# Paged value matmuls of a decode step: four pages to four groups of 32 PSUM partitions

## The chip, the cores and the metric

The kernel runs on one core of one Trainium2 chip. The metric is the device time of one execution, in microseconds (us). Shown are three runs of the kernel before; the median counts.

## The reference

One inference step of a two-layer decoder runs a prompt of 1024 positions and 8 sample sequences through the same weights. The change touches one part of layer 0, the forgetting attention of the 8 samples (FoX, 8 heads of 64), whose keys and values lie in pages of 128 positions:

```
def _fox_sample(q, k_new, v_new, logf_new, k_pool, v_pool, lf_pool, page_table):
    ...
    v_all = jnp.concatenate([v_pool[page_table].reshape(b, past, h, d).astype(v_new.dtype), v_new], axis=1)
    ...
    sc = jnp.einsum('bqhd,bkhd->bhqk', q, k_all).astype(jnp.float32) * (FOX_HD ** -0.5)
    sc = sc + c[:, :, past:, None] - c[:, :, None, :]
    ...
    p = jax.nn.softmax(sc, axis=-1).astype(v_all.dtype)
    return jnp.einsum('bhqk,bkhd->bqhd', p, v_all).reshape(b, l, h * d)
```

Here b is 8 samples, h is 8 heads, d is 64, and the past is 16 pages a sample, 128 pages in all. The change concerns the last line: probabilities times value pages.

## The kernel before, in words

The program is written by hand for five engines, each with its own list of instructions, joined by semaphores. SyncE (SP) issues most loads, TensorE (PE) does the matmuls, VectorE (DVE), ScalarE (ACT) and GpSimd (POOL) the rest. The instruction order on every engine is the order in which the code is written.

Layer 0 projects the inputs (`pe_ab_in`), turns and pools (`pe_naturals`, `pe_pool`), and then comes the stage of the change, `pe_attention` (L1133) with `act_attention`, `dve_attention`, `pool_attention` and, on SP, `sp_pages` (L944). Two pieces of work are woven together there:

- **Prompt attention** in 64 tiles (8 heads by 8 query blocks), pipelined over three rounds of a loop in n: round n has `pe_scores(n+1)` (L849), `pe_turn(n-1)` (eight transposes at most, L894) and `pe_values(n-2)` (L911). A tile of block i covers 128(i+1) keys, so its cost grows and falls with n modulo 8.
- **Sample attention** over the pages. Pages stay in `kpage`, a ring of 4 slots with 2 pages each; a step u fills one slot. SP's `fill` waits until step u-4 has been used (`pages_used`), reads two page numbers from `page_idx` (L953) and issues two loads of 256 KB (L959). Steps 0 to 63 are key pages: POOL multiplies them (L981), DVE reduces them (L987), in rounds 0 to 47. In round 48 the softmax over all samples makes the probabilities `sc`. Steps 64 to 127 are value pages, in rounds 50 to 65, four steps (eight pages) a round, after the prompt tile's own matmuls.

A sample has 16 value pages, so two rounds make one sample. `pe_sample_values` (L1052) multiplies a page of 128 positions by 512 columns with the 8 heads' probabilities of this sample and sums the 16 pages in `ps[0:8, 7, :]`, 8 partitions of PSUM bank 7. Each head's row then holds all 512 columns, of which its own 64 are wanted: `dve_sample_own` (L1065) multiplies by the mask `own` (ones in head h's 64 columns), `pe_sample_columns` (L1073) sums the 8 rows into 4 columns of 128 with ones as the moving operand, and `dve_sample_columns` (L1079) copies them out. The next sample's first page waits for that copy, since all use bank 7.

All of these matmuls are float32. The trace has two records, each with a weight load of its own, for each matmul of the program: 256 for the 128 pages.

POOL builds `own` in round 8 (`pool_own`, L1110) in 8 partitions of `w_pl`, which is free by then.

Of the kernel before, what the change touches and what calls it, by code (L numbers as in the profile page):

```python
# [24 lines left out]
ALU = mybir.AluOpType  # L25
# [6 lines left out]
P = 128  # L32
# [29 lines left out]
def hybrid_step(nc, A, O):  # L62

    with ExitStack() as ctx:
# [7 lines left out]
        def sb(name, shape, dt=F32, at=None):  # L72
            return (at or ctx).enter_context(nc.sbuf_tensor(name, shape, dt))

        def scratch(name, shape):
# [24 lines left out]
            "p (a n) -> p a n", a=4)  # L100
        smx = sb("smx", [P, DECB, 2, MH])
        sel_b = sb("sel_b", [MH * DECB, DECB])
        smr = sb("smr", [P, 4, DECB, MH])
        dskip = sb("dskip", [P, DC])
        s_new = sb("s_new", [P, 4, DECB])
# [15 lines left out]
        w_pl = sb("w_pl", [P, 4, P], F32, rest)  # L121
        lf_pg = sb("lf_pg", [P, DECB, NPG, FH], F32, rest)
        ulast = sb("ulast", [PBUF, FW], F32, rest)
        own = w_pl[0:FH].rearrange("p g n -> p (g n)")
        rest.close()
        rest = ExitStack()
        xin = sb("xin", [P, 2, D], F32, rest)
# [100 lines left out]

        STEPS = {
            "pe": ("colsT_ready", "gate_logits0", "gate_logits1", "gate_logits2", "gate_turned", "gate_sums",  # L230
                    "gate_rowsT", "stateT_ready", "ulastT_ready", "s_natT_ready", "s_values_ready",
                    "convT_turned", "dt_logits0", "dt_logits1", "dt_logits2", "dt_turned", "dt_sums",
                    "dt_rowsT", "tailT_ready", "s_bcT_ready", "lastT_ready", "wmT_turned", "v_rowT"),
            "act": ("gate_rows0", "gate_rows1", "gate_rows2", "gate_ln", "gate_token_rows", "ulast_ready",
                    "s_nat_ready", "sc_exp", "convT_ready", "dt_rows0", "dt_rows1", "dt_rows2", "dt_ln",
                    "dt_token_rows", "s_decay_ready", "ctail_ready", "s_bc_ready", "last_ready", "g_mean_sq",
                    "g_std", "v_row_ready", "rms_rstd"),
            "dve": ("inv_cnt_ready", "sel_b_ready", "gate_biased", "logf_ready", "c_ready", "new_scores",
                    "sc_cleared", "s_max_ready", "sc_shifted", "s_sum_ready", "sc_ready", "dt_biased",
                    "da_ready", "dec_diff", "g_var", "wmT_ready", "xdt_s"),  # L240
            "pool": ("own_ready", "s_max_all", "s_sum_all"),
        }
        pe_steps, act_steps, dve_steps, pool_steps = (sem(f"{e}_steps") for e in ("pe", "act", "dve", "pool"))
        marked = {e: 0 for e in STEPS}
# [805 lines left out]


        def pe_sample_values(pe, u):  # L1052
            b, slot = u // (NPG // 2), u % 4
            pe.wait_ge(page_loaded[slot], 32 * ((N_STEP + u) // 4 + 1))
            if u == 0:
                pe.wait_ge(dve_steps, step("sc_ready"))
                pe.wait_ge(sem("suffix_copied"), 8)
            if u % (NPG // 2) == 0 and b:
                pe.wait_ge(sem("s_own_step"), 2 * b)
            for e in range(2):  # L1060
                g = 2 * (u % (NPG // 2)) + e
                mm = pe.matmul(ps[0:FH, 7, :], sc[:, b, :, g], kpage[:, slot, e], start=(g == 0), stop=(g == NPG - 1))  # L1062
            mm.then_inc(pages_used, 1)

        def dve_sample_own(dve, b):  # L1065
            if b == 0:
                dve.wait_ge(pool_steps, step("own_ready"))
# [42 lines left out]
        def pool_own(pool):  # L1110
            then = chain(pool, "pool")
            pool.wait_ge(sem("pool_copied"), 4)
            then(pool.memset(own, 1.0))
            then(pool.affine_select(out=own, in_=own, compare_op=ALU.is_ge, fill=0.0, base=0,
                                    pattern=[[1, FW]], channel_multiplier=-FD))
            pool.affine_select(out=own, in_=own, compare_op=ALU.is_ge, fill=0.0, base=FD - 1,
                               pattern=[[-1, FW]], channel_multiplier=FD).then_inc(pool_steps, mark("own_ready"))

        def pool_attention(pool):
            pool.sem_inc(pages_used, 4)  # L1120
# [12 lines left out]
        def pe_attention(pe):  # L1133
            pe.wait_ge(set_free[0], G1["ab_u"])
            pe.wait_ge(act_steps, step("s_nat_ready"))
            pe.wait_ge(sem("v_copied"), NT)
            pe.wait_ge(act_steps, step("ulast_ready"))
            pe.wait_ge(sem("pool_copied"), 4)
            pe_scores(pe, 0)
            for n in range(N_ATT + 2):  # L1140
                if n + 1 < N_ATT:
                    pe_scores(pe, n + 1)
                if 1 <= n <= N_ATT:
                    pe_turn(pe, n - 1)
                if n >= 2:
                    pe_values(pe, n - 2)
                if 8 <= n < 12:
                    pe_suffix(pe, n - 8)
                if sample_done(n) is not None:
                    pe_sample_columns(pe, sample_done(n))  # L1150
                for u in value_steps(n):
                    pe_sample_values(pe, u)
            pe_sample_columns(pe, DECB - 1)
            pe_sample_new(pe)

        def act_attention(act):
            for n in range(N_ATT + 2):
                if n < N_ATT:
                    act_exp(act, n)
                    if n % NT == NT - 1 and n // NT + 2 < FH:  # L1160
                        act_load_c(act, n // NT + 2)
                if 1 <= n <= N_ATT:
                    act_turn(act, n - 1)
                if n >= 2:
                    act_out(act, n - 2)
                if n == KEYS_END:
# [1396 lines left out]
```

## Time and profile before

| | us |
|---|---|
| three runs | 4037.15, 4042.88, 4042.89 |
| median | 4042.88 |
| span of the profiled execution | 4042.7 |
| prompt tiles with key pages, about 315 to 502 | 187 |
| prompt tiles with value pages, 528.5 to 696.5 | 168 |

The profile is one execution; its span is 0.2 us under the median of the runs, and its own time is one of that size. TensorE is busy for 89% of the span and holds 73% of the chain of work that ended last. Layer 0's output projection follows the stage of the change and starts on TensorE at 702.4 us. Where the profile gives a granted clock, 1.00 is 2.4 GHz and 0.50 is 1.2 GHz; a stretch in between has some of both.

### The profile page before, as it was taken

Reading aid. Unit: us, or ns where it says so; the run is one execution under the profiler, and the core shown is the slowest. Engines: PE = TensorE matmul, PEld = TensorE weight load, DVE = VectorE, ACT = ScalarE, POOL = GpSimd, SP = SyncE. Lnnn points to the kernel's source line nnn. Section 1 sums busy time; section 2 is a strip of 40 time slices with the busy share of each in tenths; the row PEclk is TensorE's granted clock in tenths of the full one; section 3 lists DMA queues with packets and bytes.
Section 4 is the critical chain, followed back from the end, with each engine's and each line's share of the span. In section 5 each row is a group of like instructions: output and inputs, shape, how many; then the busy total and the mean of one; then the engine's idle time right before and its main releaser. Section 6 shows DMA issues by size and latency. Waiting matters only on the chain.

```text
span 4042.7 us, 55900 instructions
## 1 busy us (share of the span) xinstructions
PE 3584.0 (89%) x21060; PEld 3248.2 (80%) x21060; DVE 1514.9 (37%) x2160; ACT 1005.0 (25%) x1325; POOL 586.3 (15%) x367
## 2 busy tenths in 40 slices
PE   7978899979988999999779986668899799999996
PEld 6955533969778999999778975658896799999996
DVE  1159922442444212222431438654343522221225
ACT  2123321142323101111232323432332311111112
POOL 2337700210022000000220014002100300000003
PEclk9977899999999999999889998889999899999997
DMA  2235655133411111111122112331352111111111
GB/s 82 54 107 162 185 162 171 57 109 106 144 42 34 45 47 47 42 47 43 30 68 71 47 44 89 126 120 52 104 171 75 30 47 47 43 45 47 47 35 54
DMA packets 370178, 311.19 MB, mean 77 GB/s; under 512 B 23520, under 2 KB 312721, under 8 KB 369923
## 3 DMA queue, kind: packets, MB, share of 16 engines
q1 hardware_dynamic: 354351, 291.40, 23.9%
q10 hardware_dynamic: 11620, 17.77, 1.3%
q0 software_dynamic: 4096, 0.53, 0.2%
q8 instruction: 71, 1.16, 0.1%
q14 instruction: 40, 0.33, 0.0%
HBM read 283.46 MB, written 26.51 MB: 77 GB/s over the span
## 4 chain that ended last, share of the span: by engine, by line
PE 73%; DVE 11%; issue 5%; DMA 4%; POOL 3%; ACT 3%; SPq 2%; ACTq 0%; DVEq 0%; POOLq 0%
PE ps L302 62%; PE ps L1062 2%; POOL kpage L981 2%; PE ps L1494 1%; PE ps L1516 1%; DVE spl_w L287 1%; PE ps L1472 1%; DVE acc L2111 1%; PE ps L600 1%; DMA acc<-spill_d 1%; DVE x L1289 1%; SPq L953 1%; DMA raw_w<-in_w_xv 1%; ACT x L1303 1%; POOL x L1295 1%
## 5 line engine op out<-in xcount | busy, mean ns | idle before, releaser
L302 PE MATMUL ps<-xs,spl_w 128*128 128x344 f32 x12528 | 2006.8, 323 | 53.4 <-DVE spl_w L287 25.2
L302 PEld LDWEIGHTS ps<-xs,spl_w 128*128 128x128 f32 x12528 | 2000.8, 190 | 57.5 <-issue 27.2
L287 DVE TENSOR_TENSOR spl_w<-raw_w,spl_w 128x1024 fp32r<-128x1024 f32 x268 | 327.1, 1220 | 839.5 <-ACT spl_w L283 835.5
L302 PE MATMUL ps<-hs,spl_w 128*128 128x344 f32 x3168 | 512.5, 325 | 27.5 <-DVE hs L1707 27.5
L302 PEld LDWEIGHTS ps<-hs,spl_w 128*128 128x128 f32 x3168 | 510.9, 192 | 29.0 <-issue 29.0
L283 ACT CAST spl_w<-raw_w 128x1024 fp32r<-128x1024 f32 x268 | 279.4, 1042 | 390.6 <-PE ps L302 362.6
L1243 POOL MEMSET sum_x<- 128x1032 f32 x6 | 5.9, 982 | 1739.2 <-DVE hs L1707 1374.0
L1705 DVE TENSOR_TENSOR sum_x<-sq,ps 128x1032 f32<-128x1032 f32 x44 | 54.1, 1229 | 351.5 <-PE ps L302 351.5
L1251 POOL TENSOR_TENSOR sum_x<-sum_x,x 128x1032 f32<-128x1032 f32 x48 | 115.9, 2414 | 474.7 <-DVE x L1211 188.1
L1295 POOL TENSOR_TENSOR x<-x,sum_x 128x1032 f32 x48 | 138.5, 2893 | 200.4 <-DVE x L1289 200.4
L981 POOL TENSOR_TENSOR kpage<-kpage,qb 128x1024 f32<-128x1024 f32 x64 | 156.3, 2459 | 65.5 <-DMA kpage<-in_cache_fox_k 65.3
L1689 ACT CAST hs<-sum_x 128x1032 f32 (+1 forms) x44 | 46.4, 1055 | 472.2 <-DVE sum_x L1705 472.2
L1211 DVE SCALAR_TENSOR_TENSOR x<-x,ps 128x1032 f32 (+1 forms) x48 | 58.9, 1228 | 267.9 <-PE ps L302 267.9
L1229 ACT ACTIVATE sq<-x 128x1032 f32 (+1 forms) x48 | 51.2, 1067 | 420.7 <-DVE x L1211 233.9
L1220 DVE TENSOR_TENSOR sum_sq<-sum_sq,sq 128x1032 f32<-128x1032 f32 x48 | 106.7, 2223 | 92.6 <-ACT sq L1229 60.3
L1213 DVE TENSOR_TENSOR x<-x,ps 128x1032 f32 (+1 forms) x40 | 49.2, 1229 | 242.4 <-PE ps L302 242.4
L317 PE MATMUL ps<-xs,spl_w 128*128 128x344 f32 x432 | 78.8, 342 | 62.1 <-DVE xs L1307 62.1
L302 PE MATMUL ps<-mem_s,spl_w 128*128 128x256 f32 x768 | 103.6, 294 | 32.6 <-DVE spl_w L287 17.0
L1685 ACT ACTIVATE sq<-ps 128x1032 f32<-128x1032 f32 x44 | 45.4, 1032 | 339.9 <-PE ps L302 336.2
L302 PEld LDWEIGHTS ps<-mem_s,spl_w 128*128 128x128 f32 x768 | 98.0, 199 | 39.4 <-DVE spl_w L287 19.8
L317 PEld LDWEIGHTS ps<-xs,spl_w 128*128 128x128 f32 x432 | 73.8, 203 | 67.9 <-issue 47.2
L1062 PE MATMUL ps<-kpage,sc 128*8 128x512 f32 x256 | 113.4, 592 | 5.3 <-DMA kpage<-in_cache_fox_v 2.8
(344 smaller groups left out, 3224.1 us busy)
## 6 DMA issues: line engine op xcount, KB each, us to landing
kpage<-in_cache_fox_k SPq DMA_DIRECT2D x128, 256.0 KB, 2.9
kpage<-in_cache_fox_v SPq DMA_DIRECT2D x128, 256.0 KB, 2.9
raw_w<-in_w_gate SPq DMA_DIRECT2D x44, 512.0 KB, 3.8
raw_w<-in_w_up SPq DMA_DIRECT2D x44, 512.0 KB, 3.8
mkv<-in_cache_mem_k SPq DMA_DIRECT2D x16, 1024.0 KB, 8.2
mkv<-in_cache_mem_v SPq DMA_DIRECT2D x16, 1024.0 KB, 5.1
raw_w<-in_w_down SPq DMA_DIRECT2D x32, 512.0 KB, 3.8
raw_w<-in_w_in_cd SPq DMA_DIRECT2D x28, 512.0 KB, 3.8
```

The lines of the kernel that those rows point to most:

```text
L283: act.copy(spl_w[:, s, 0], raw_w[:, s]).then_inc(hi_ready, 1)
L287: dve.tensor_tensor(spl_w[:, s, 1], raw_w[:, s], spl_w[:, s, 0].bitcast(F32), ALU.subtract).then_inc(lo_ready, 1)
L302: mm = pe.matmul(ps[:, 3 * s + t, 0:width], spl_w[:, s, a, k], part[:, k, width * t:width * (t + 1)], start=(k == 0 and step == 0), stop=( ...
L317: mm = pe.matmul(ps_set[s][:, t], spl_w[:, s, a, k], act_in[:, b, k, TB * t:TB * (t + 1)], start=(k == 0 and step == 0), stop=(k == DC - 1 ...
L981: pool.tensor_tensor(kpage[:, slot], kpage[:, slot], qb[:, b % 2].unsqueeze(1).to_broadcast([P, 2, FW]), ALU.mult).then_inc(sem("keys_mult ...
L1062: mm = pe.matmul(ps[0:FH, 7, :], sc[:, b, :, g], kpage[:, slot, e], start=(g == 0), stop=(g == NPG - 1))
L1211: ins = dve.scalar_tensor_tensor(out=xm, in0=xm, scalar=ALPHA, in1=ps_set[s], op0=ALU.mult, op1=ALU.add)
L1220: dve.tensor_tensor(sum_sq[:], sum_sq[:], sq[:], ALU.add).then_inc(sem("sq_used"), 1)
L1229: act.activation(sq[:], chunk(x, 2 * i + s), ACT.Square).then_inc(sem("sq_ready"), 1)
L1251: pool.tensor_tensor(sum_x[:], sum_x[:], chunk(x, 2 * i + s), ALU.add).then_inc(sem("sum_x_ready"), 1)
L1295: pool.tensor_tensor(xk, xk, sum_x[:], ALU.add).then_inc(sem("ln_shifted"), 1)
L1705: dve.tensor_tensor(blocks(sum_x[:]), blocks(sq[:]), ps_set[1], ALU.mult).then_inc(set_free[1], 1)
```

## The change

Four pages go through TensorE together. Page j of the four writes PSUM partitions 32j to 32j+31 of bank 7. For that the stationary operand has 32 columns, the 8 heads of four samples (the sample's own and three others), where it had the 8 heads of one. Each group of 32 partitions sums 4 of the sample's 16 pages. Afterwards the mask `own` covers 128 partitions, head h's 64 columns repeated in every eighth row, and `sel_row[:, b % 4]`, a column that is 1 in the 8 rows of sample b in each group and 0 in the 24 others, takes the place of the ones in the summing matmul.

A call of `pe_sample_values` now takes two slots: it waits for both, issues four matmuls and frees the first slot after the second and the second after the fourth. SP's program is unchanged.

Added are two small DVE operations at the start (`sel_row`, `head_of`) and, in round 20, one matmul (`pe_own`) and one ACT copy of 128x512 (`act_own`), which spread POOL's 8 rows of the mask over 128 partitions. The first value page now waits for ACT's copy, and DVE's first masking too, where it waited for POOL.

```diff
-        own = w_pl[0:FH].rearrange("p g n -> p (g n)")
+        own = w_pl[:].rearrange("p g n -> p (g n)")
...
+            dve.tensor_reduce(sel_row[:], ident[:].rearrange("p (j m h) -> p m j h", j=4, h=FH), AX.XY, ALU.add
+                              ).then_inc(dve_steps, mark("sel_row_ready"))
+            dve.tensor_copy(head_of[:].rearrange("p (r h) -> p r h", h=FH),
+                            ident[0:FH, 0:FH].unsqueeze(1).to_broadcast([FH, P // FH, FH])
+                            ).then_inc(dve_steps, mark("head_of_ready"))
...
         def pe_sample_values(pe, u):
-            b, slot = u // (NPG // 2), u % 4
-            pe.wait_ge(page_loaded[slot], 32 * ((N_STEP + u) // 4 + 1))
+            b = u // (NPG // 2)
+            for v in (u, u + 1):
+                pe.wait_ge(page_loaded[v % 4], 32 * ((N_STEP + v) // 4 + 1))
             if u == 0:
+                pe.wait_ge(act_steps, step("own_ready"))
...
-            for e in range(2):
-                g = 2 * (u % (NPG // 2)) + e
-                mm = pe.matmul(ps[0:FH, 7, :], sc[:, b, :, g], kpage[:, slot, e], start=(g == 0), stop=(g == NPG - 1))
-            mm.then_inc(pages_used, 1)
+            for j in range(4):
+                g = 2 * (u % (NPG // 2)) + j
+                mm = pe.matmul(ps[32 * j:32 * (j + 1), 7, :], sc[:, 4 * (b // 4):4 * (b // 4 + 1), :, g],
+                               kpage[:, (u + j // 2) % 4, j % 2], start=(g < 4), stop=(g >= NPG - 4))
+                if j % 2:
+                    mm.then_inc(pages_used, 1)
...
-            dve.tensor_tensor(qb[0:FH, b % 2], ps[0:FH, 7, :], own, ALU.mult).then_inc(sem("s_own_step"), 1)
+            dve.tensor_tensor(qb[:, b % 2], ps[:, 7, :], own, ALU.mult).then_inc(sem("s_own_step"), 1)
...
-                mm = pe.matmul(ps[:, 7, c:c + 1], qb[0:FH, b % 2, P * c:P * (c + 1)], ones[0:FH, 0:1], start=True, stop=True)
+                mm = pe.matmul(ps[:, 7, c:c + 1], qb[:, b % 2, P * c:P * (c + 1)], sel_row[:, b % 4:b % 4 + 1], start=True, stop=True)
...
+        def pe_own(pe):
+            pe.wait_ge(pool_steps, step("own_rows"))
+            pe.wait_ge(dve_steps, step("head_of_ready"))
+            pe.wait_ge(sem("suffix_copied"), 8)
+            pe.matmul(ps[:, 7, :], head_of[:], own[0:FH], start=True, stop=True).then_inc(pe_steps, mark("own_spread"))
+
+        def act_own(act):
+            act.wait_ge(pe_steps, step("own_spread"))
+            act.copy(own, ps[:, 7, :]).then_inc(act_steps, mark("own_ready"))
...
-                for u in value_steps(n):
+                if n == 20:
+                    pe_own(pe)
+                for u in value_steps(n)[::2]:
                     pe_sample_values(pe, u)
```

On TensorE, round 52 of the stage stood so before: the sums of the sample that has just ended (L1076), then four steps of two pages (L1062), each with a wait of its own, then the scores of the next tile (L849).

```order
L1076 MATMUL ps<-ones,qb 128x1 [waits s_own_step]
L1076 MATMUL ps<-ones,qb 128x1 x3
L1062 MATMUL ps<-kpage,sc 8x512 [waits s_own_step,page_loaded0]
L1062 MATMUL ps<-kpage,sc 8x512
L1062 MATMUL ps<-kpage,sc 8x512 [waits page_loaded1]
L1062 MATMUL ps<-kpage,sc 8x512
L1062 MATMUL ps<-kpage,sc 8x512 [waits page_loaded2]
L1062 MATMUL ps<-kpage,sc 8x512
L1062 MATMUL ps<-kpage,sc 8x512 [waits page_loaded3]
L1062 MATMUL ps<-kpage,sc 8x512
L849 MATMUL ps<-proj 128x512 [waits scores_shifted]
```

The same round in the changed kernel, where L1087 is the sum, L1071 the values and L856 the scores:

```order
L1087 MATMUL ps<-sel_row,qb 128x1 [waits s_own_step]
L1087 MATMUL ps<-sel_row,qb 128x1 x3
L1071 MATMUL ps<-kpage,sc 32x512 [waits s_own_step,page_loaded1,page_loaded0]
L1071 MATMUL ps<-kpage,sc 32x512 x3
L1071 MATMUL ps<-kpage,sc 32x512 [waits page_loaded3,page_loaded2]
L1071 MATMUL ps<-kpage,sc 32x512 x3
L856 MATMUL ps<-proj 128x512 [waits scores_shifted]
```

There are as many matmuls as before, with 32 output rows for 8, in two groups of four pages in place of four of two; the waits of two slots have moved to the head of each group.

In round 20, in the stage of the key pages, TensorE's list has one new row (L1135) between the tile's values (L918) and the next tile's scores (L856); before, the second followed the first.

```order
L901 MATMUL ps<-ident,prob 128x128 x3
L918 MATMUL ps<-pT,proj 64x128 [waits out_copied,pT_copied]
L918 MATMUL ps<-pT,proj 64x128 x2
L1135 MATMUL ps<-w_pl,head_of 128x512 [waits suffix_copied,dve_steps,pool_steps]
L856 MATMUL ps<-proj 128x512 [waits scores_shifted]
L856 MATMUL ps<-proj 128x384
```

Behind that row the tile's next scores wait for POOL's mask rows and for DVE's copies out of bank 7, both of rounds up to 12.

## Rows read from the trace of the kernel before

**Rows 1.** The page: span, TensorE's busy time, and the chain that ended last.

```profile
span 4042.7 us, 55900 instructions
...
PE 73%; DVE 11%; issue 5%; DMA 4%; POOL 3%; ACT 3%; SPq 2%; ACTq 0%; DVEq 0%; POOLq 0%
PE ps L302 62%; PE ps L1062 2%; POOL kpage L981 2%; PE ps L1494 1%; PE ps L1516 1%; DVE spl_w L287 1%; PE ps L1472 1%; DVE acc L2111 1%; PE ps L600 1%; DMA acc<-spill_d 1%; DVE x L1289 1%; SPq L953 1%; DMA raw_w<-in_w_xv 1%; ACT x L1303 1%; POOL x L1295 1%
```

**Rows 2.** Groups by line, value stretch: count | busy us, mean ns | idle before.

```profile
L1062 PE MATMUL ps<-kpage,sc 128*8 128x512 f32 x256 | 113.4, 592 | 5.3 <-DMA kpage<-in_cache_fox_v 2.8 <-DVE s_sum L1081 2.4
L1062 PEld LDWEIGHTS ps<-kpage,sc 128*8 128x8 f32 x256 | 22.0, 92 | 84.0 <-issue 73.8 <-DMA kpage<-in_cache_fox_v 10.2
...
L1071 DVE TENSOR_TENSOR qb<-ps,w_pl 8x512 f32<-8x512 f32 x8 | 5.4, 679 | 73.6 <-PE ps L1062 73.6
```

**Rows 3.** TensorE in order of time: start, us, what, [idle before].

```profile
528.49 7.04 PE L1062 MATMUL ps<-kpage,sc 128*8 128x512 f32 x16
...
567.94 1.98 PE L849 MATMUL ps<-proj 64*128 64x512 f32 x4
...
571.89 1.05 PE L1076 MATMUL ps<-ones,qb 8*128 8x1 f32 x8
573.29 7.03 PE L1062 MATMUL ps<-kpage,sc 128*8 128x512 f32 x16 [0.35 <-DVE s_sum L1081]
...
611.63 1.12 PE L849 MATMUL ps<-proj 64*128 64x512 f32 x2
...
613.41 1.05 PE L1076 MATMUL ps<-ones,qb 8*128 8x1 f32 x8
```

**Rows 4.** SP in order of time: all issues of value pages behind the first eight.

```profile
531.25 160.93 SPq L959 DMA_DIRECT2D kpage<-in_cache_fox_v  x120
```

**Rows 5.** SP's waits, 505 to 702 us: total, times, longest.

```profile
SPq L953 <- PE ps L1062: 21.6, 5, 17.1
```

**Rows 6.** Chain in order of time, 505 to 705 us: two turns of SP's loop, the end.

```profile
671.21 0.25 issue
...
681.71 0.25 issue
...
691.84 2.69 DMA kpage<-in_cache_fox_v
694.58 1.90 PE ps L1062 x4
```

**Rows 7.** TensorE in layer 1, two heads that meet in 64 columns each.

```profile
2456.61 0.38 PE L2147 MATMUL ps<-xbc,hprev 128*64 128x128 f32 x2
2456.83 0.44 PE L2145 MATMUL ps<-acc,xdt 128*64 128x128 f32 x4
2457.05 0.27 PE L2147 MATMUL ps<-xbc,hprev 128*64 128x128 f32 x1
2457.10 0.27 PE L2145 MATMUL ps<-acc,xdt 128*64 128x128 f32 x1
2457.16 0.27 PE L2147 MATMUL ps<-xbc,hprev 128*64 128x128 f32 x1
2457.21 0.27 PE L2145 MATMUL ps<-acc,xdt 128*64 128x128 f32 x1
```

**Rows 8.** Stretches: length, PE, PEld, DVE, ACT, POOL busy, granted clock, DMA share, GB/s.

```profile
315.00:502.00 187.00, 155.84 (x679) 98.66 (x679) 174.04 (x349) 70.22 (x162) 143.36 (x63) 0.79 0.57 175
528.00:697.00 169.00, 163.21 (x567) 57.87 (x565) 28.94 (x106) 25.78 (x57) 0.16 (x1) 1.00 0.63 187
702.00:706.00 4.00, 3.63 (x13) 3.66 (x14) 4.00 (x5) 4.00 (x5) 0.00 (x0) 0.50 0.00 0
```

**Rows 9.** ACT's copies of 128x512 out of PSUM: min, median, max ns, first and last start.

```profile
L724 ACT COPY kst<-ps x8: 585/585/586, 239.1 to 250.7; 128x512 f32<-128x512 f32 x8
```

**Rows 10.** VectorE in order of time at the start of the program.

```profile
5.69 0.12 DVE L452 TENSOR_REDUCE sel_b<-ident 32x8 f32<-32x32 f32 x1
50.00 1.23 DVE L287 TENSOR_TENSOR spl_w<-raw_w,spl_w 128x1024 fp32r<-128x1024 f32 x1 [44.19 <-ACT spl_w L283]
```

More of the change, by code:

```diff
@@ L102, in hybrid_step @@
         sel_b = sb("sel_b", [MH * DECB, DECB])
+        sel_row = sb("sel_row", [P, 4])
+        head_of = sb("head_of", [FH, P])
         smr = sb("smr", [P, 4, DECB, MH])
@@ L230, in hybrid_step @@
             "pe": ("colsT_ready", "gate_logits0", "gate_logits1", "gate_logits2", "gate_turned", "gate_sums",
-                    "gate_rowsT", "stateT_ready", "ulastT_ready", "s_natT_ready", "s_values_ready",
+                    "gate_rowsT", "stateT_ready", "ulastT_ready", "s_natT_ready", "own_spread", "s_values_ready",
                     "convT_turned", "dt_logits0", "dt_logits1", "dt_logits2", "dt_turned", "dt_sums",
@@ L234, in hybrid_step @@
             "act": ("gate_rows0", "gate_rows1", "gate_rows2", "gate_ln", "gate_token_rows", "ulast_ready",
-                    "s_nat_ready", "sc_exp", "convT_ready", "dt_rows0", "dt_rows1", "dt_rows2", "dt_ln",
+                    "s_nat_ready", "own_ready", "sc_exp", "convT_ready", "dt_rows0", "dt_rows1", "dt_rows2", "dt_ln",
                     "dt_token_rows", "s_decay_ready", "ctail_ready", "s_bc_ready", "last_ready", "g_mean_sq",
                     "g_std", "v_row_ready", "rms_rstd"),
-            "dve": ("inv_cnt_ready", "sel_b_ready", "gate_biased", "logf_ready", "c_ready", "new_scores",
+            "dve": ("inv_cnt_ready", "sel_b_ready", "sel_row_ready", "head_of_ready", "gate_biased", "logf_ready", "c_ready", "new_scores",
                     "sc_cleared", "s_max_ready", "sc_shifted", "s_sum_ready", "sc_ready", "dt_biased",
                     "da_ready", "dec_diff", "g_var", "wmT_ready", "xdt_s"),
-            "pool": ("own_ready", "s_max_all", "s_sum_all"),
+            "pool": ("own_rows", "s_max_all", "s_sum_all"),
         }
@@ L1059, in pe_sample_values @@
                 pe.wait_ge(sem("s_own_step"), 2 * b)
-            for e in range(2):
-                g = 2 * (u % (NPG // 2)) + e
-                mm = pe.matmul(ps[0:FH, 7, :], sc[:, b, :, g], kpage[:, slot, e], start=(g == 0), stop=(g == NPG - 1))
-            mm.then_inc(pages_used, 1)
+            for j in range(4):
[4 more added lines that the diff above has]
+                    mm.then_inc(pages_used, 1)
         def dve_sample_own(dve, b):
             if b == 0:
-                dve.wait_ge(pool_steps, step("own_ready"))
+                dve.wait_ge(act_steps, step("own_ready"))
             dve.wait_ge(pages_used, N_STEP + 4 + (NPG // 2) * (b + 1))
@@ L1112, in pool_own @@
             pool.wait_ge(sem("pool_copied"), 4)
-            then(pool.memset(own, 1.0))
-            then(pool.affine_select(out=own, in_=own, compare_op=ALU.is_ge, fill=0.0, base=0,
+            rows = own[0:FH]
+            then(pool.memset(rows, 1.0))
+            then(pool.affine_select(out=rows, in_=rows, compare_op=ALU.is_ge, fill=0.0, base=0,
                                     pattern=[[1, FW]], channel_multiplier=-FD))
-            pool.affine_select(out=own, in_=own, compare_op=ALU.is_ge, fill=0.0, base=FD - 1,
-                               pattern=[[-1, FW]], channel_multiplier=FD).then_inc(pool_steps, mark("own_ready"))
+            pool.affine_select(out=rows, in_=rows, compare_op=ALU.is_ge, fill=0.0, base=FD - 1,
+                               pattern=[[-1, FW]], channel_multiplier=FD).then_inc(pool_steps, mark("own_rows"))
+        def pe_own(pe):
[6 more added lines that the diff above has]
+            act.copy(own, ps[:, 7, :]).then_inc(act_steps, mark("own_ready"))
         def pool_attention(pool):
@@ L1165, in act_attention @@
                     act_out(act, n - 2)
+                if n == 20:
+                    act_own(act)
                 if n == KEYS_END:
```

## The prediction

> **What bounds the kernel now.** I read the page first. TensorE is busy for 89% of a span of 4042.7 us and holds 73% of the chain, but the line that the change speeds up, L1062, has only 2% of the chain [rows 1]. So I left the whole program and looked at its stretch, 528 to 697 us, by groups. There L1062 has 256 records and 113.4 us of 169, at the full clock, and TensorE is busy for 163 of the 169 [rows 2, 8]. By that view the stretch is TensorE's. The timeline gives the real rate: 16 records in 7.04 us, so 0.44 us from one start to the next (the mean of 592 ns counts a tail that overlaps the next), 0.88 us a page and 1.76 us a step of two pages [rows 3]. All 128 pages are 112.6 us.
>
> The next view turns this over. SP issued the last 120 value pages from 531.25 on, over 160.9 us with the last issue's own 0.34 us, 160.6 from first start to last [rows 4]. One turn of its loop is eight pages: two marks of a turn stand at 671.21 and 681.71, 10.50 us apart [rows 6]. Fifteen turns are 157.5 us; the last turn ends at its eighth issue and not at the next turn's first, 1.7 us less, so 155.8. SP therefore lost only 160.6 - 155.8 = 4.8 us. The view of its waits agrees: 21.6 us on L1062 in five waits, of which one of 17.1 us lies before 531, while the ring was full and nothing had been used; 4.5 us are left for the other four [rows 5]. So two engines are almost level: SP takes 10.5 us for the eight pages of a round, and TensorE 7.0 us for their matmuls beside 1.8 to 5.4 us for the rest of the round. The ring of four slots hides the one behind the other. The chain ends on SP: last load issued at 691.84, landed 2.7 us later, two pages' matmuls of 1.90 us [rows 6], then the mask and the sums. DMA is no third limit, at 0.63 of its time [rows 8].
>
> **The change part by part.** The numbers go against this execution's own span of 4042.7 us; the median of the three runs is 4042.88, so I write the result against that.
>
> *The four matmuls.* A page keeps its two records, 0.43 to 0.44 us apart. The trace of before has no four matmuls in four groups of 32 columns. Its nearest row is in layer 1, where one head's matmuls write partitions 0 to 63 and the next head's 64 to 127: two records of one head take 0.38 us, each 0.27 long, 0.11 apart, but where two heads meet the starts are 0.05 to 0.06 apart, 2457.05, 2457.10, 2457.16, 2457.21 [rows 7]. Both halves stream at their own full rate. With four such groups, four pages take 2 x 0.44 + 0.15 (the tail of the last) = 1.05 us; two at a time 4 x 0.44 + 0.15 = 1.9; one after the other 8 x 0.44 + 0.15 = 3.7. I take 1.1, since [rows 7] show independent column groups at work, and keep 3.7 as the far end. The stage's L1062 time falls from 113 to some 35 us. The wider weight load (32 columns for 8, 92 ns before [rows 2]) lies under the matmul ahead.
>
> *What this is worth.* Not 78 us, for SP is unchanged: 155.8 us from its first issue to its last. The most that can be gained is: SP's stalls, 4.8; the first slots come free after 1.1 us and not 1.76, 0.7; and behind the last landing four pages take 1.1 us and not two pages 1.9, 0.8. Together **6.3 us**, if no new stall comes.
>
> *The pairing.* A group needs two slots, and the ring has two groups. SP takes 5.25 us for a group of four pages. From the landing of a group's last page to the moment at which SP wants its first slot back I count 5.25 (the next group) + 1.3 (its next issue) - 2.9 (landing) - 1.0 (530.25, when the first step ended, to the issue at 531.25 [rows 3, 4]) = 2.6 us. TensorE is away for the tile's own matmuls meanwhile: 3.95 us in the longest round (567.94 to 571.89), and in every second round 1.05 for the sums and 0.35 for their copy, 5.35 in all [rows 3]. A group that lands 5.25 us after the one before was landed and used 1.1 later is used 1.1 + 5.35 + 1.1 - 5.25 = 2.3 us after landing. That is just under 2.6: at the full clock the pairing costs nothing or a few tenths.
>
> *The clock.* In the value stretch TensorE never rested and had 1.00. In the stretch of the key pages, with the same prompt tiles and pauses between them, it had 0.79 on the mean [rows 8], that is 42% of the time at 1.2 GHz. After the change a round is 10.5 us with about 2.9 + 0.7 + 2.2 = 5.8 us of work on TensorE, so pauses come back, and I expect the same fall. At 1.2 GHz a round of the longest kind takes 2 x (3.95 + 1.05 + 2.1) + 0.35 = 14.5 us, 4.0 more than SP's 10.5; of the shortest even kind (1.78 us from 611.63 to 613.41) 2 x (1.78 + 1.05 + 2.1) + 0.35 = 10.2. By the mean of the two ends the seven rounds with sums would be 1.85 us too long each, 13 us in all, and 28 if all were of the longest kind; rounds without sums fit on the mean (12.1 and 7.8 by the same ends). I take 17 us if the whole stretch ran so, nearer the mean. At 42% of it 7 us; but short slow spells are in part taken up by the ring, and a round at the full clock catches up. Bounds 0 and 7; I take half, **3.5 us**.
>
> *The rest.* `pe_own` is one matmul of 512 columns, 0.9 us by the same spacing, and ACT's copy 0.59 us [rows 9]. They stand in the key stretch, where POOL and DVE are busy 77% and 93% [rows 8] and TensorE and ACT wait; the next scores and the next exponential are behind them, so between 0 and 1.5 us, say **1**. The mask on DVE has 128 partitions for 8 with the same 512 columns, 0.68 us [rows 2]; eight sums keep their shape but for the rows. The two small DVE operations fall into a wait of 44 us that ends at 50.00, and one like them took 0.12 us [rows 10]: nothing. The new wait of the first value page on ACT's copy ended some 30 rounds ago. The projection behind the stretch starts at 0.50 of the clock already [rows 8], so a low clock at the end costs it nothing more.
>
> *Sum.* -6.3 + 3.5 + 1 = -1.8 us: 4042.9 - 1.8 = **4041.1 us**. A measurement of this kernel can tell about 0.2% from no change, 8.1 us; this is well inside.
>
> **The rivals.**
>
> *The clock holds.* If the matmuls of four pages count as work enough and 1.00 stays, the whole 6.3 us come, less the 1 us: 4037.6. For it: with some 5.8 us of work in 10.5, the pauses are cut in short pieces. Against it: in the key stretch TensorE is busy for 156 of 187 us and the clock fell all the same [rows 8]. Still within 0.2% of before.
>
> *One after the other.* The change doesn't do what it says if column groups with a common set of rows run in turn. Then TensorE has its old work and the coarser ring: a group lands 5.25 - 3.7 = 1.6 us behind the use of the last, and its first step is used 5.35 + 1.76 - 1.6 = 5.5 us after landing, 2.9 too late, in the longest round; 0.7 in the shortest; over seven such rounds some 12 us of stalls for the 4.8 of before, and 1.8 us more at the end: +9, 4052. It decides as soon as four pages take over 2.5 us. What [rows 7] show speaks against it, though with two groups and not four. The Trainium skill, "TensorE: Matmul & The Clock Gate", Part 3 under "The mechanism", speaks for it: a weight load overlaps matmuls in flight only where the row group differs, and here all four pages use all 128 rows. By that rule each of eight loads would show too, with 0.09 us apiece a group of 4.4 us (an estimate), and the time would be this rival's and not the sum's. The trace does not agree: a load that waited for the other half's matmuls, 0.27 us long, would keep the starts apart, and they come 0.05 us apart [rows 7].
>
> *The clock stays low.* If 1.2 GHz lasts nearly through the stretch, the 17 us above stand against 6.3 gained, with 1 for the key stretch: +12, 4055. It decides where rounds of 12 to 14 us follow each other. For it: in the key stretch the low clock went on while TensorE was busy 156 of 187 us. Against it: such a stretch is busy all the time, and the same clock rose again and again there.
>
> *TensorE is the limit after all.* Then the 78 us saved would show: 3965. SP's times speak against it [rows 4, 6]; it would have to issue twice as fast. The skill's "TensorEngine Tiling (Array Packing)", under "Theoretical Speedup", gives up to 4x for 32 columns; that is this rival's gain on L1062, and by my sum it is there and not worth having.
>
> **How the numbers follow.** Forecast 0.52, the clock holds 0.18, one after the other 0.13, the clock stays low 0.14, TensorE the limit 0.03. The forecast's own range, with clock costs of 0 to 7 and pages two at a time, is 4036 to 4047. To leave out no more than 2 in 10 it must take in 4052 and most of the slow clock: 4035 to 4054. Faster by over 0.2%: the last rival and a little of the second, 0.07. Slower: most of the two slow ones, 0.20. The rest, 0.73, is within.
>
> **What would show it.** Right: SP's 120 issues in 156 to 161 us, with TensorE idle before the value matmuls and a DMA named as the releaser; starts of four pages about 0.1 us apart; the clock between 0.6 and 0.9. Wrong: starts of the value matmuls 0.44 us apart throughout; SP's waits on them over 10 us behind the first; or an SP loop whose turn is well off 10.5 us.

## The result, and the profile after

The changed kernel takes 4056.92 us (median of 20 runs, 4049.34 to 4066.28), the kernel before 4042.89 on the same chip (20 runs, 4032.93 to 4051.63). The ratio is 1.0035, with a 95% interval of 1.0028 to 1.0042: **slower by 14 us**. The prediction said no measurable change, 4041.1, with a range up to 4054. The profiled execution has a span of 4056.0 us, 13.3 more than before.

The value matmuls first. TensorE's groups by line, 528 to 715 us (columns as in [rows 2]), and VectorE's masking in the view by line:

```profile
L1071 PE MATMUL ps<-kpage,sc 128*32 128x512 f32 x256 | 52.2, 916 | 49.6 <-DMA kpage<-in_cache_fox_v 47.1 <-DVE s_sum L1092 2.4
```

```profile
L1082 DVE TENSOR_TENSOR qb<-ps,w_pl x8: 690/691/693, 547.6 to 712.3; 128x512 f32<-128x512 f32 x8
```

The 256 records are busy for 52.2 us where they were 113.4 [rows 2]: the part that was to become quick did. In front of them TensorE now waits 47.1 us for loads, where it was 2.8. The mask costs 0.69 us for 0.68, as forecast.

TensorE in order of time, two pieces of the stretch (columns as in [rows 3]):

```profile
569.52 1.94 PE L1071 MATMUL ps<-kpage,sc 128*32 128x512 f32 x8 [2.63 <-DMA kpage<-in_cache_fox_v]
571.39 3.78 PE L856 MATMUL ps<-proj 64*128 64x512 f32 x4
...
578.42 1.05 PE L1087 MATMUL ps<-sel_row,qb 128*128 128x1 f32 x8
579.83 1.95 PE L1071 MATMUL ps<-kpage,sc 128*32 128x512 f32 x16 [0.35 <-DVE s_sum L1092]
...
588.54 1.94 PE L1071 MATMUL ps<-kpage,sc 128*32 128x512 f32 x8 [3.98 <-DMA kpage<-in_cache_fox_v]
593.64 1.94 PE L1071 MATMUL ps<-kpage,sc 128*32 128x512 f32 x8 [3.16 <-DMA kpage<-in_cache_fox_v]
```

At the full clock eight pages take 1.95 us (579.83), where 16 records took 7.04 [rows 3]; at half of it four pages take 1.94. So four groups of columns do run beside each other. The Trainium skill, "TensorE: Matmul & The Clock Gate", Part 3 under "The mechanism", lets a weight load overlap only matmuls of another row group; that rule, taken alone, would have these four pages, which share all rows, run in turn. The trace doesn't agree: 1.95 us for eight pages has no room for it. But the quick groups now wait for loads (2.63, 3.98, 3.16), and the prompt's scores behind one of them take 3.78 us for four records where the same shape took 1.98 [rows 3].

The clock by stretches says why: the stretch of [rows 8], then one of 120 us that lies inside the value stretch of every kernel below (length, busy PE, PEld, DVE, ACT, POOL, granted clock, DMA share, GB/s):

```profile
528.00:697.00 169.00, 126.55 (x540) 61.14 (x538) 28.91 (x105) 26.49 (x59) 2.35 (x1) 0.64 0.58 171
537.00:657.00 120.00, 89.50 (x363) 41.37 (x363) 20.76 (x78) 17.74 (x41) 0.00 (x0) 0.63 0.60 180
```

Before, the same two stood at 1.00. At a mean of 0.64, TensorE is at 1.2 GHz for 72% of the time ((1 - 0.64) / 0.5). The same page of the Trainium skill, Part 1 under "HAM oscillation — how this bites in real kernels", tells of a kernel whose short groups of matmuls wait for loads in between and start each time at the low clock. The trace agrees in part: the three groups behind waits of 2.6 to 4.0 us take 1.94 us each, the time of the low clock, while the eight pages at 579.83, which follow prompt work and sums without a wait for loads, run at the full one.

SP, its value loads in order of time and its waits from 505 to 725 us, answers to [rows 4, 5]:

```profile
533.84 173.66 SPq L966 DMA_DIRECT2D kpage<-in_cache_fox_v  x120
```

```profile
SPq L960 <- PE ps L1071: 33.9, 8, 15.7
```

The first wait, 15.7, is the full ring before the first use. The other seven are 18.2 us, where four had 4.5. One by one they are 3.0, 3.1, 2.4, 1.1, 3.1, 5.3 and 0.2 us, and each stands before the issue that needs the slot of a new sample's first page: they fall in the seven rounds with the sums, the rounds that the prediction had found too long at 1.2 GHz. SP's loop needs 173.3 us from first start to last, 17.5 over the 155.8 of an SP that never waits: the waits account for all of it. The chain at the end, as in [rows 6]:

```profile
707.16 2.95 DMA kpage<-in_cache_fox_v
710.25 2.00 PE ps L1071 x8
712.27 0.70 DVE qb L1082
713.02 1.88 PE ps L1087 x8
```

The value stretch (first value matmul to the end of the last) lasts 180.3 us for 168.0. The 13.3 us of the span are: 3.4 by which it starts later (531.9 for 528.5), 12.3 by which it is longer, 1.1 between its end and the output projection (7.0 us for 5.9; the last sums, 713.02, take 1.88 us at the low clock, where 578.42 has 1.05 at the full one), and 3.5 less in the rest of the program: 3336.8 us for 3340.3. That rest is 3336.8 us in e5 below too, which has the matmuls of before, so the 3.5 us are not shown to be the change's.

### The profile page after: what moved, and what is told of

Its sections match the earlier page's. It is cut to its first block, busy times and chain, and to the rows that moved or that the text cites. A ratio compares the mean times of both kernels' runs of the same rounds, so it can differ in the third digit from the quotient of the medians.

```text
span 4056.0 us, 55933 instructions
## 1 busy us (share of the span) xinstructions
PE 3558.2 (88%) x21062; PEld 3255.4 (80%) x21062; DVE 1516.4 (37%) x2162; ACT 1005.7 (25%) x1326; POOL 586.3 (14%) x367
## 4 chain that ended last, share of the span: by engine, by line
PE 73%; DVE 10%; issue 5%; DMA 4%; ACT 3%; POOL 2%; SPq 2%; ACTq 0%; DVEq 0%; POOLq 0%
PE ps L304 62%; PE ps L1520 1%; PE ps L1542 1%; PE ps L856 1%; PE ps L918 1%; POOL kpage L988 1%; SPq L960 1%; DVE spl_w L289 1%; DMA raw_w<-in_w_xv 1%; DVE x L1315 1%; DVE acc L2137 1%; PE ps L607 1%; DMA acc<-spill_d 1%; PE ps L1071 1%; PE ps L1498 1%
## 5 line engine op out<-in xcount | busy, mean ns | idle before, releaser
L304 PE MATMUL ps<-mem_s,spl_w 128*128 128x256 f32 x768 | 101.4, 290 | 34.0 <-DVE spl_w L289 18.2
L856 PE MATMUL ps<-proj 64*128 64x512 f32 (+2 forms) x192 | 118.0, 740 | 1.4 <-ACT proj L819 1.3
```

Of the source, the lines that this page charges most:

```text
L304: mm = pe.matmul(ps[:, 3 * s + t, 0:width], spl_w[:, s, a, k], part[:, k, width * t:width * (t + 1)], start=(k == 0 and step == 0), stop=( ...
L856: mm = pe.matmul(score_ps[n % 2][:, k0:k1], proj[r, h // 2, P * i:P * (i + 1)], proj[r, 4 + h // 2, k0:k1], start=True, stop=True)
```

## The experiments

The theory after this reading: TensorE got quick, so it waited, so its clock fell; at 1.2 GHz the prompt tiles keep it from the pages, slots come back late, and SP, which sets the pace, loses 18 us. The rival: the pairs do it, whatever the clock (a pair is the two slots that one group of four pages waits for together, half of the ring). A second rival was the spreading of the mask. In all experiments the stretch is read from the first value matmul to the end of the last; medians and ratios stand against the kernel before, run beside it on the same chip (4037.99 us for e1 to e4, 4038.61 for e5 to e8, 4038.03 for e9 to e12). The stretch belongs to one profiled execution, the ratio to all runs; where they differ, the ratio is the verdict. Line numbers shift with the edits.

### e1: each slot by itself

```diff
-            for v in (u, u + 1):
-                pe.wait_ge(page_loaded[v % 4], 32 * ((N_STEP + v) // 4 + 1))
+            pe.wait_ge(page_loaded[u % 4], 32 * ((N_STEP + u) // 4 + 1))
...
             for j in range(4):
+                if j == 2:
+                    pe.wait_ge(page_loaded[(u + 1) % 4], 32 * ((N_STEP + u + 1) // 4 + 1))
```

> Four column groups as in the changed kernel, but each slot is waited for and freed by itself, in steps of two pages as before the change. Clock theory (in the value stretch TensorE ran at 1.2 GHz 72% of the time, so the prompt tiles between the pages took twice as long and slots came free late): the pauses stay, the granted clock stays at 0.6 to 0.75, SP waits 10 us or more on the value matmuls behind its first wait, 4050 to 4057 us. Pairing theory (two slots at once make the ring too coarse): SP's waits fall to 5 us or less, about 4040 us.

Measured: 4043.12 us, ratio 1.0016 (1.0006 to 1.0026), stretch 167.5 us. By stretch, and SP's waits:

```profile
537.00:657.00 120.00, 99.90 (x389) 41.07 (x389) 21.46 (x79) 17.81 (x40) 0.00 (x0) 0.74 0.66 192
```

```profile
SPq L960 <- PE ps L1072: 20.9, 4, 15.7
```

Without pairs SP loses 5.2 us behind its first wait for 18.2, about what it lost before the change. That is what the pairing theory had for the waits; the clock theory's 10 us and its 4050 to 4057 us did not come. But the kernel is still slower than before, and the clock stands at 0.74, so the clock isn't independent of the pairs. By the ratio about half of the loss is left. The one profile doesn't show where: its stretch is 0.5 us under that of before; the stretch starts 2.6 us later and 1.1 us more lie behind it.

### e2: the pairs at the full clock, with slow groups

```diff
-                mm = pe.matmul(ps[32 * j:32 * (j + 1), 7, :], sc[:, 4 * (b // 4):4 * (b // 4 + 1), :, g],
-                               kpage[:, (u + j // 2) % 4, j % 2], start=(g < 4), stop=(g >= NPG - 4))
+                mm = pe.matmul(ps[0:32, 7, :], sc[:, 4 * (b // 4):4 * (b // 4 + 1), :, g],
+                               kpage[:, (u + j // 2) % 4, j % 2], start=(g == 0), stop=(g == NPG - 1))
```

Mask and sums take 32 rows. All else stays, the pairs too.

> Pairs of slots as in the changed kernel, but all four pages go to the first 32 partitions one after the other, so TensorE has the streaming time of before (0.44 us a record). Clock theory: without pauses the clock stays at 1.00 in the value stretch and the time is that of before, 4040 to 4046 us, SP's waits about 5 us. Pairing theory: the clock is 1.00 too, but SP waits 12 us or more behind its first wait, about 4052 us.

Measured: 4051.27 us, ratio 1.0035 (1.0020 to 1.0049), stretch 177.6 us.

```profile
537.00:657.00 120.00, 112.18 (x379) 45.77 (x378) 22.18 (x85) 19.37 (x44) 0.00 (x0) 0.99 0.63 186
```

```profile
SPq L960 <- PE ps L1071: 29.0, 8, 16.7
```

```profile
583.97 3.65 PE L1071 MATMUL ps<-kpage,sc 128*32 128x512 f32 x8
```

Four pages in turn take 3.65 us, 3.3 times the 1.09 of four groups at this clock (the rows of e3). The clock stays at 0.99 and SP loses 12.3 us behind the first wait. This is what the pairing theory had (12 us or more, about 4052), and the clock theory's 4040 to 4046 failed. So pairs cost as much at the full clock, if TensorE is late for another reason: here too, pairing turned lateness of TensorE into lost time of SP.

### e3: filler work in the changed kernel

```diff
                 if j % 2:
                     mm.then_inc(pages_used, 1)
+            if u % 4 == 0:
+                for _ in range(3):
+                    pe.matmul(ps[0:1, 7, :], later[:, P - 1:P], proj[:, 12, 0:512], start=False, stop=False)
```

Three matmuls a round whose one column of weights is zero, so they add nothing to the sums.

> The changed kernel, and after the first group of four pages in each round three matmuls of 512 columns with a column of zeros as weights, added to partition 0 of bank 7, 2.6 us of streaming at 2.4 GHz in which TensorE otherwise waited for the next pages. Clock theory: the granted clock of the value stretch goes from 0.64 to 0.9 or more, SP's waits fall to 5 us or less, 4037 to 4044 us, so more work makes it faster. Pairing theory: more work on TensorE can only free slots later, 4057 us or more.

Measured: 4035.41 us, ratio 0.9993 (0.9984 to 1.0002), stretch 164.3 us.

```profile
537.00:657.00 120.00, 97.72 (x481) 39.47 (x482) 22.66 (x82) 19.46 (x44) 0.00 (x0) 0.94 0.67 199
```

```profile
SPq L960 <- PE ps L1071: 15.9, 1, 15.9
```

TensorE in order of time, a round of e3:

```profile
574.98 1.09 PE L1071 MATMUL ps<-kpage,sc 128*32 128x512 f32 x8 [0.40 <-DMA kpage<-in_cache_fox_v]
...
581.25 1.10 PE L1071 MATMUL ps<-kpage,sc 128*32 128x512 f32 x8 [2.39 <-DMA kpage<-in_cache_fox_v]
582.13 2.74 PE L1077 MATMUL ps<-proj,later 128*1 128x512 f32 x6
586.14 1.09 PE L1071 MATMUL ps<-kpage,sc 128*32 128x512 f32 x8 [1.26 <-DMA kpage<-in_cache_fox_v]
```

With 2.74 us of useless work a round (582.13) the ratio falls from 1.0035 to 0.9993, 0.42% or 17 us. The clock is at 0.94, SP waits for no slot behind the first, and the pairs are all still there. With e1 and e2 this says how the two work together: **with quick groups and a clock near the full one the pairs cost next to nothing; what the change brought is the low clock, which makes TensorE late, and the pairs pass the lateness on to SP.** No run has single slots at a clock of 0.63, so what the low clock costs without pairs isn't shown.

### e4: without the spreading of the mask

`pe_own` and `act_own` are left out, so rows 8 to 127 of the mask hold other data, and the samples' attention output becomes other numbers, with the same work.

> The changed kernel without spreading the mask: no matmul and no ACT copy in round 20, so rows 8 to 127 of the mask hold other numbers and the samples' attention output is not the reference's. If the spreading delayed the key stretch (its last key page was used about 3 us later than before), this is 3 to 4 us faster than the changed kernel, about 4053 us, and the value stretch starts at 528 to 529 us. If that delay was the chance of the clock in the key stretch, it is within 1 us of the changed kernel, 4056 to 4058 us.

Measured: 4057.84 us, ratio 1.0036 (1.0023 to 1.0049); the stretch starts at 535.8.

```profile
537.00:657.00 120.00, 90.01 (x368) 41.26 (x361) 20.36 (x78) 17.28 (x40) 0.00 (x0) 0.63 0.62 178
```

The loss and the clock are those of the changed kernel: the spreading is not the cause, nor of the later start. (A cost of 1 us could not be seen: the interval is 10 us wide.) The traces say the same of the start. Here are, from TensorE in order of time, the scores of one and the same prompt tile in the kernel before, the changed kernel and e2, whose program is the changed one's up to there, and then the matmul of the spreading in the changed kernel:

```profile
334.96 1.34 PE L849 MATMUL ps<-proj 64*128 64x512 f32 x4
```

```profile
339.85 1.34 PE L856 MATMUL ps<-proj 64*128 64x512 f32 x4
```

```profile
334.42 1.34 PE L856 MATMUL ps<-proj 64*128 64x512 f32 x4
```

```profile
390.19 2.07 PE L1135 MATMUL ps<-w_pl,head_of 8*128 8x512 f32 x2
```

The changed kernel was 4.9 us behind some 50 us before the spreading ran, and e2 was 0.5 us ahead with the same program.

### e9 and e10: is the low clock a habit, and does the dose count?

e9 is the changed kernel again; e10 is e3 with `range(1)` for `range(3)`.

> The changed kernel once more, unaltered, so that its own spread is known: its profiled execution had a value stretch of 180 us at 0.65 of the clock, and one execution is one draw. If the low clock is the kernel's habit and not that execution's, the stretch is again 174 to 184 us, the clock in it 0.6 to 0.75, and the ratio to the kernel before 1.002 to 1.005. If it was chance, the stretch is under 172.

> e3 with one filler matmul a round in place of three. Theory (idle time of TensorE lowers the clock): less work in the same pauses gives a clock between the 0.65 of none and the 0.95 of three, and a stretch between 180 and 164 us. Rival (it is not the work but the place of the three matmuls, behind the round's first group): the whole gain stays, 162 to 166 us.

Measured: e9 4054.11 us, ratio 1.0035 (1.0022 to 1.0049), stretch 177.1 us; e10 4042.88 us, ratio 1.0007 (0.9997 to 1.0016), stretch 174.1 us. The stretches, first e9's, then e10's:

```profile
537.00:657.00 120.00, 89.41 (x360) 42.35 (x361) 20.77 (x78) 16.85 (x39) 0.00 (x0) 0.63 0.60 181
```

```profile
537.00:657.00 120.00, 91.48 (x404) 41.95 (x404) 22.40 (x85) 19.37 (x44) 0.00 (x0) 0.77 0.63 187
```

The clock of 0.63 came again, and one filler lies between none and three in clock, stretch and time. But e10's profiled execution, 4053.51 us, is the slowest of its twelve, so its clock and stretch are not those of its median. By the ratio one filler brings 11 of the 17 us, and its interval overlaps that of e3: that more work gives more is likely from the clocks, 0.63, 0.77 and 0.94, and not settled by the times.

### e8: filler and single slots together

e1 and e3 in one kernel, the filler behind every second group.

> The filler matmuls of e3 together with the single slots of e1. Theory: at the full clock the pairing costs nothing, so this stands within 2 us of e3 (ratio to the kernel before 0.998 to 1.000), its stretch at 162 to 165 us. Rival, clock and pairing are two separate costs that add: it stands 6 to 9 us under e3.

Measured: 4036.20 us, ratio 0.9999 (0.9988 to 1.0010), stretch 161.9 us.

```profile
537.00:657.00 120.00, 103.33 (x482) 41.64 (x481) 23.74 (x87) 19.89 (x45) 0.00 (x0) 1.00 0.69 200
```

```profile
531.38 156.38 SPq L966 DMA_DIRECT2D kpage<-in_cache_fox_v  x120
```

Level with e3, as the theory had it; two costs that add would have shown 6 to 9 us. SP's 156.0 us from first start to last are the 155.8 of the prediction's SP that never waits, and the stretch is 6.1 us under that of before: this is the ceiling. In the time it isn't seen: the ratio allows for a gain of at most 0.12%.

### e5 to e7: SP's limit taken away

For value steps 4 to 63 SP loads the first page of a slot, and POOL the second on its own queue, with semaphores of its own (some others are shared to make room). e5 is the kernel before with this edit, e6 the changed kernel, e7 is e1 with it:

```diff
-                    fill(slot, N_STEP + 4 * m + slot, 2 * (4 * m + slot), A["cache_fox_v"])
+                    fill(slot, N_STEP + 4 * (m + 1) + slot, 2 * (4 * (m + 1) + slot), A["cache_fox_v"], (0,))
...
+        def pool_values(pool):
+            for u in range(4, N_STEP):
+                pool.wait_ge(pages_used, N_STEP + u + 1)
+                page = pool.value_load(page_idx[0:1, 2 * u + 1:2 * u + 2], min_val=0, max_val=NPHYS - 1)
+                pool.dma_start(kpage[:, u % 4, 1], A["cache_fox_v"][0, ds(page, 1)].rearrange("a t h d -> (a t) (h d)")
+                               ).then_inc(sem(TOO[u % 4]), 16)
```

> The kernel before; for value steps 4 to 63 SP issues the first page of each slot and POOL the second, on a queue of its own (semaphores of its own, and other semaphores shared so that enough are left). Theory: in the kernel before SP (10.50 us a round of eight pages) and TensorE (163 of 169 us busy at the full clock) are almost level in the value stretch; with SP's issuing halved TensorE is the limit, and at most 6 us can be gained: the stretch falls from 168 to 162 to 166 us, the time by 2 to 6 us, and the clock stays at 1.00. Rival, SP alone is the limit: the stretch falls by over 20 us.

> The changed kernel with the same two queues. Theory: what the four-way matmuls save on TensorE is hidden behind SP's issuing, so with half of it moved to POOL the stretch falls until the next limit, the DMA engines (0.63 of 169 us before, some 106 us of transfers) or POOL's own issuing, of which no row here tells the length: a stretch of 106 to 135 us for 180, so 45 to 75 us faster than the changed kernel and 30 to 60 faster than before. TensorE has some 93 us of work at the full clock in it, so the clock should stand higher than the 0.65 of the changed kernel. Rival, the low clock of TensorE with its prompt tiles is the limit now: at 1.2 GHz throughout its work is some 160 us and the gain over before is under 10 us.

> The changed kernel with the two queues, each slot waited for and given back by itself as in e1. Theory, pairing costs where loads are the limit and TensorE is late: 0 to 9 us faster than e6, and nothing between the two if the DMA engines are the limit and the ring is always full.

Measured: e5 4040.02 us, ratio 1.0002 (0.9992 to 1.0011), stretch 164.2; e6 4029.56 us, ratio 0.9973 (0.9963 to 0.9984), stretch 154.1; e7 4009.65 us, ratio 0.9931 (0.9913 to 0.9949), stretch 131.2. The stretches of e5, e6 and e7:

```profile
537.00:657.00 120.00, 117.91 (x411) 42.90 (x410) 23.77 (x87) 19.99 (x44) 23.86 (x44) 1.00 0.59 195
```

```profile
537.00:657.00 120.00, 93.74 (x418) 46.21 (x416) 23.08 (x86) 20.42 (x46) 25.95 (x48) 0.69 0.62 205
```

```profile
537.00:657.00 120.00, 98.86 (x525) 46.92 (x523) 26.59 (x98) 24.20 (x53) 31.23 (x59) 0.94 0.75 250
```

The kernel before gains nothing that shows from a second queue, where 2 to 6 us were expected (the interval leaves room for 3): TensorE is busy for 117.9 of 120 us. So both limits of the kernel before were real and level. The quick groups are worth their time only where loads come faster. But e6 fell short of its 106 to 135 us and came out near its rival, a gain over before of under 10 us: the clock again, 0.69, against which e7 has 0.94. That e7 beat e6 by 20 us, where 0 to 9 were expected, could be the single slots or the clock; the next two tell.

### e11 and e12: two queues with the filler

> e6 (two queues, pairs) with the three filler matmuls a round. If e6 was held at 153.6 us by its clock of 0.70, the filler brings 0.9 or more, and the stretch falls towards the 131 of e7: 128 to 140 us, 10 to 25 us faster than e6. If e6 was held by the pairs alone (two slots of a ring of four come back at one time, and the loads wait for them), the filler adds 2.7 us a round in the way of that and the stretch is 150 to 175 us.

> e7 (two queues, single slots) with the three filler matmuls a round. Its clock stood at 0.94 already, so there is little to win: 16 rounds with up to 2.7 us of filler each, of which part lies in waits for loads. Stretch 131 to 155 us for 131, 0 to 24 us slower than e7. If the clock of e7 was a lucky draw, the filler holds it and the times are level.

Measured: e11 4006.59 us, ratio 0.9915 (0.9900 to 0.9930), stretch 132.7; e12 4002.90 us, ratio 0.9918 (0.9902 to 0.9935), stretch 132.2. First e11, then e12:

```profile
537.00:657.00 120.00, 112.31 (x607) 49.10 (x600) 27.85 (x101) 25.06 (x55) 30.83 (x56) 1.00 0.74 242
```

```profile
537.00:657.00 120.00, 115.42 (x606) 52.42 (x604) 25.62 (x91) 22.81 (x49) 29.42 (x54) 1.00 0.74 244
```

Filler work takes 21 us off the stretch of e6, and with pairs or single slots the result is the same, 132.7 and 132.2. All in one table:

| loads by | slots | filler matmuls | clock 537 to 657 | stretch, us | ratio to before |
|---|---|---|---|---|---|
| SP | pairs | 0 (the change) | 0.63 | 180.3 | 1.0035 |
| SP | pairs | 1 (e10, its slowest execution) | 0.77 | 174.1 | 1.0007 |
| SP | pairs | 3 (e3) | 0.94 | 164.3 | 0.9993 |
| SP | single | 0 (e1) | 0.74 | 167.5 | 1.0016 |
| SP | single | 3 (e8) | 1.00 | 161.9 | 0.9999 |
| SP and POOL | pairs | 0 (e6) | 0.69 | 154.1 | 0.9973 |
| SP and POOL | pairs | 3 (e11) | 1.00 | 132.7 | 0.9915 |
| SP and POOL | single | 0 (e7) | 0.94 | 131.2 | 0.9931 |
| SP and POOL | single | 3 (e12) | 1.00 | 132.2 | 0.9918 |

e7, e11 and e12 beat both kernels, by 28 to 35 us under the kernel before; among the three the intervals don't tell. What holds the stretch at 131 to 133 us wasn't tried further. DMA stands at 0.74 to 0.75 in all three, TensorE at 99 to 115 of 120 us with the filler counted in. TensorE's waits for loads from 537 to 657 us, in e7, e11 and e12:

```profile
PE ps L1088 <- DMA kpage<-in_cache_fox_v: 18.4, 20, 2.0
```

```profile
PE ps L1087 <- DMA kpage<-in_cache_fox_v: 4.8, 8, 1.5
```

```profile
PE ps L1088 <- DMA kpage<-in_cache_fox_v: 0.6, 2, 0.3
```

With the filler TensorE hardly waits for loads any more: there it is TensorE with its useless work that sets the pace. Without it, in e7, loads still hold it up for 18.4 us.

## Why the prediction was wrong

**Right: SP sets the pace, and the 78 us saved on TensorE don't show.** e8 ran SP at 156.0 us, the forecast's 155.8, and its stretch gained 6.1 us against the ceiling of 6.3, too little to be seen in the time. e5 and e7 show the other side: a second queue is worth nothing to the kernel before, and with quick groups in single slots the time is 28 us under it.

**Right: four pages in 1.1 us.** 1.09 at the full clock, 1.94 at the low one. The rival "one after the other" fell with that row; e2 built it, and SP then lost 12.3 us behind its first wait for the 12 that the rival had; its time was 13 us over before, for the rival's 9. The Trainium skill's "TensorEngine Tiling (Array Packing)", under "Theoretical Speedup", has up to 4x for 32 columns; the trace has 3.65 / 1.09, or 3.3.

**Right near the full clock, as far as the runs tell: the pairing costs nothing or a few tenths.** In e3, with pairs at 0.94, SP waited for no slot behind the first, and its time is level with that of e8, single slots at 1.00; the stretches are 2.4 us apart. (e11 and e12, 0.5 us apart at 1.00, say less: TensorE sets the pace there, and not the loads.) The 0.3 us of slack that the prediction found (2.3 against 2.6) fits e3, but it is so small that a slower TensorE uses it up, as in e2 and in the changed kernel.

**Wrong: the clock, 3.5 us within 0 to 7.** This is the step that failed. The prediction took the 42% at 1.2 GHz of the key stretch over to the value stretch, then 42% of 17 us, then half of that, because "short slow spells are in part taken up by the ring, and a round at the full clock catches up". The clock was low for 72% of the stretch, not 42%. And the ring didn't take it up: SP lost 18.2 us behind its first wait. Between the changed kernel and e8, the same loads at the full clock with single slots, lie 18.4 us of stretch; with pairs at 0.94 (e3) 16.0. So the 17 us that the prediction had for a stretch all at 1.2 GHz was nearly the whole bill, at 72%. The way in which it thought the low clock would cost was right: the seven waits of SP lie in the seven rounds with the sums. What failed is how long the clock would be low, and the halving. With 16.0 to 18.4 in place of 3.5 its sum would be +11 to +13, and the two measurements of the kernel both have a ratio of 1.0035, +14. The prediction had named the sign: waits of SP over 10 us behind the first.

The reason given against a lasting low clock was that the key stretch is busy all the time and the clock rose there again and again. But the key stretch had TensorE busy for 156 of 187 us (0.83) and a clock of 0.79, and the value stretch after the change for 126.6 of 169 (0.75) and a clock of 0.64, most of that at the durations of 1.2 GHz. The prediction's own 5.8 us of work in a round of 10.5 are 0.55: it saw much more rest coming than the stretch had from which it took its 42%, and took the 42% all the same. And a loop may close there that the prediction left out: at the low clock slots come back late, loads come late, TensorE waits longer, and the clock stays low. The clock of 0.74 in e1, with single slots and no other change, speaks for it; no run shows the loop by itself.

**The rival "the clock stays low" is what came**: 4055 with a chance of 0.14, and 4056.9 measured. The range was cut at 4054, just under it. That the rival's number fits so well is in part luck: its 17 us were for a stretch nearly all at 1.2 GHz, and they came at 72%.

**Small terms.** The spreading was put at 1 us within 0 to 1.5; its matmul took 2.07 us for the 0.9 of the sum, and leaving it out (e4) gains nothing that can be seen. The first release came 0.8 us sooner after the first use in e8 (531.38 against a start at 529.4; before, 531.25 against 528.5), for the 0.7 of the sum. That a low clock at the end costs nothing more was off by 1.1 us.

Open: the value stretch started between 526.2 and 536.8 us in the fourteen profiles, with a clock of 0.71 to 0.77 from 300 to 500 us; the changed kernel's two executions are at 531.9 and 532.0, the kernel before at 528.5 and e5 at 526.5. Whether the 3 to 4 us are the change's isn't settled: e2 and e12, with the same key stretch as the changed kernel, started at 528.5 and 526.2. It isn't the spreading, since e4 started at 535.8 and the changed kernel was late before it.

## What to carry to other kernels

Before you make an engine quicker that isn't the only limit, ask what it will do with the time: here TensorE came to wait for loads, the granted clock of its stretch fell from 1.00 to 0.63 for everything else in it too, and a saving of 60 us of work became a loss of 14. Where two engines are level, free both together: the quick matmuls alone cost 14 us and the second queue alone gained nothing, both together gained 28 to 35, once filler or single slots kept the clock up (11 without). A slack that holds only at the full clock (0.3 us of a round here) is to be worked out at the low one too, and if wait times are left over, cheap work in them can be worth more than none (17 us in e3).

## What the runs showed of the hardware that was not expected

- Matmuls with a single stationary column, 2.74 us in a round of some 10, lifted the granted clock from 0.63 to 0.94 (e3) and, with two queues, from 0.69 to 1.00 (e11). One third of them gave 0.77 in the one execution profiled (e10).
- The clock reaches back into the loads: with the same list of loads and the same two queues the DMA engines moved 205 GB/s at a clock of 0.69 and 242 at 1.00 (e6, e11).
- POOL, with its page number read and a wait in between, started loads 1.15 us apart when nothing held it up, SP 1.31 (10.50 us for eight). POOL in order of time, e7:

```profile
536.60 0.54 POOL L991 DMA_DIRECT2D kpage<-in_cache_fox_v  x1 [0.42 <-issue]
537.74 0.54 POOL L991 DMA_DIRECT2D kpage<-in_cache_fox_v  x1 [0.60 <-issue]
538.89 0.54 POOL L991 DMA_DIRECT2D kpage<-in_cache_fox_v  x1 [0.61 <-issue]
```
